# Expert weights in 16 KB runs, TensorE's order inside an expert turn rotated, the token copy split

## What is computed

```python
N_EXPERTS, TOP_K, EXPERT_FF = 32, 2, 512
# hier_moe: softmax over 4 groups, best group, two best experts in it; weights w
def expert_block(args):
    xblk, e = args
    return (jax.nn.silu(xblk @ w_gate[e]) * (xblk @ w_up[e])) @ w_down[e]
# the outputs, times their routing weights, are added up for each token
```

## Time and profile before

| | |
|---|---|
| median of 3 runs | 2574.07 us (2572.4 to 2574.95) |
| span of the profiled execution | 2569.7 us |
| mean granted TensorE clock | 0.941 |
| PE busy, DVE busy, ACT busy | 2164.8 us, 826.1 us, 386.2 us |
| HBM read, written | 606.41 MB, 30.93 MB |
| expert weight loads | 198 of 2048 KB |
| stores to `y_rows` from SBUF | 132 of 128 KB, 5.5 us to landing |
| L680 MATMUL (up) | x2112, 489.5 us busy, mean 617 ns |
| L699 MATMUL (down) | x1056, 241.2 us busy, mean 597 ns |
| L659 MATMUL (tokens) | x1696, 202.1 us busy, mean 280 ns |

### The profile page before, as it was taken

The page is one execution under the profiler, slowest core; times in us unless marked ns, Lnnn a source line. Parts: engine busy times, 40 slices in busy tenths (PEclk is TensorE's granted clock), DMA queues, the critical chain, the costliest instruction groups (busy, mean ns, idle before and its releaser), DMA issues. The chain is left out here.

```text
span 2569.7 us, 27407 instructions
## 1 busy us (share of the span) xinstructions
PE 2164.8 (84%) x10510; PEld 1378.6 (54%) x10514; DVE 826.1 (32%) x1726; ACT 386.2 (15%) x724; POOL 113.9 (4%) x56
## 2 busy tenths in 40 slices
PE   7789998978999893697999888885989788888874
PEld 6578887667888641444444444444546433333332
DVE  1456663045666529023111111113073311111112
ACT  1321111042111210420000000002122100000000
POOL 0000000000000008500000000001000000000000
PEclk9899999999999897898999999997989899999997
DMA  7536656312766643014999999987121599999994
GB/s 253 196 112 253 224 201 248 139 50 82 260 230 221 221 180 130 0 66 177 397 397 397 396 397 397 397 316 247 66 99 66 194 396 396 397 397 397 396 396 149
DMA packets 273636, 638.07 MB, mean 248 GB/s; under 512 B 7120, under 2 KB 10224, under 8 KB 273456
## 3 DMA queue, kind: packets, MB, share of 16 engines
q1 hardware_dynamic: 256096, 595.48, 62.3%
q0 software_dynamic: 5600, 21.27, 2.3%
q10 hardware_dynamic: 11888, 20.62, 2.2%
HBM read 606.41 MB, written 30.93 MB: 248 GB/s over the span
## 5 line engine op out<-in xcount | busy, mean ns | idle before, releaser
L680 PE MATMUL T<-ring,S 128*64 128x512 f32 x2112 | 489.5, 617 | 75.1 <-issue 68.8
L680 PEld LDWEIGHTS T<-ring,S 128*64 128x64 f32 x2112 | 179.9, 142 | 376.9 <-issue 373.8
L561 PE MATMUL T<-X,ring 128*128 128x256 f32 x1536 | 338.9, 380 | 0.0
L561 PEld LDWEIGHTS T<-X,ring 128*128 128x128 f32 x1536 | 292.4, 191 | 40.2 <-issue 0.6
L699 PE MATMUL T<-ring,S 128*64 128x512 f32 x1056 | 241.2, 597 | 40.1 <-DVE S L1465 40.1
L1463 DVE TENSOR_TENSOR S<-S,T 128x256 f32<-128x256 f32 x66 | 27.8, 422 | 727.5 <-ACT S L1056 727.5
L1267 DVE SCALAR_TENSOR_TENSOR S<-ring,cs,S 128x512 f32<-128x512 f32 x336 | 229.5, 745 | 0.0
L659 PEld LDWEIGHTS T<-S 128*128 128x128 f32 x1696 | 195.5, 195 | 41.3 <-issue 41.3
L659 PE MATMUL T<-S 128*128 128x128 f32 x1696 | 202.1, 280 | 14.3 <-DVE S L1346 14.3
L569 PE MATMUL T<-S,ring 128*128 128x256 f32 x768 | 176.7, 383 | 15.1 <-DVE S L1297 15.1
L506 PE MATMUL T<-H,ring 128*128 128x512 f32 (+1 forms) x496 | 167.7, 501 | 4.4 <-ACT H L1023 4.0
(11 more groups left out here) (269 smaller groups left out, 1565.6 us busy)
## 6 DMA issues: line engine op xcount, KB each, us to landing
ring<-in_exp_w_gate SPq DMA_DIRECT2D x66, 2048.0 KB, 18.6
ring<-in_exp_w_up SPq DMA_DIRECT2D x66, 2048.0 KB, 22.7
ring<-in_exp_w_down SPq DMA_DIRECT2D x66, 2048.0 KB, 19.9
ring<-in_ffn_w_up SPq DMA_DIRECT2D x24, 2048.0 KB, 12.7
ring<-in_mod_w SPq DMA_DIRECT2D x24, 2048.0 KB, 7.9
ring<-in_ffn_w_down SPq DMA_DIRECT2D x12, 2048.0 KB, 7.8
y_rows<-S ACTq DMA_DIRECT2D x132, 128.0 KB, 5.5
y_rows<-zb POOLq DMA_DIRECT2D x4, 3072.0 KB, 22.6
```

Of the source, the lines that this page charges most:

```text
L561: ins = pe.matmul(T[:, m % 2, h * S:(h + 1) * S], w[:, k, m * P:(m + 1) * P], x1[:, k, :], start=(k == 0), stop=(k == KT - 1))
L680: ins = pe.matmul(T[c * B:(c + 1) * B, s, :].rearrange("p (a n) -> p a n", a=2), xgT[:, k, s * B:(s + 1) * B], ring[:, 3 * s:3 * s + 2, k ...
```

## The change

- **Loads.** The DRAM side is read as `e (p k) n -> p (e k n)`: partition p takes rows 8p to 8p + 7 of gate and up (4p to 4p + 3 of down), 16 KB in one run. The bytes are the same.
- **Matching the new order of rows.** `hrow` is written permuted by ScalarE (input from PSUM with a step of 8 elements), so that token column q of tile k is input channel 8q + k. The up-projection reads its moving operand as `p g (q f) -> p g f q`: elements 16 bytes apart, so that hidden unit 4q + f comes out at column q of block f.
- **TensorE's order.** A prologue does tokens and the up-projection s = 0 of the first turn. The loop body is: transpositions (i, 0), tokens (i + 1), up (i, 1), down (i, 0), transpositions (i, 1), up (i + 1, 0), down (i, 1). An epilogue does the last turn without tokens. SyncE, ScalarE and VectorE follow the same order, with a prologue and an epilogue of their own; the count in `plan` is one lower.
- **Token copy.** The 128 x 1024 copy becomes two, one for each s, and semaphore `xT` counts two for each turn. GpSimd's wait for `xT_all` goes.

```diff
@@ -442,8 +442,8 @@
                 weights = (a["exp_w_gate"], a["exp_w_up"], a["exp_w_down"])
 
                 def load(m, w):
-                    src = w.rearrange("e (k p) n -> p (e k) n", p=P)
-                    sp_.dma_start(mslot(m, src.shape[1], src.shape[2]), src).then_inc(r["landed"][m], 16)
+                    src = w.rearrange("e (p k) n -> p (e k n)", p=P)
+                    sp_.dma_start(ring[:, m, :], src).then_inc(r["landed"][m], 16)
 
 
                 for m in (3, 4, 5, 2, 0, 1):
...
@@ -451,25 +451,37 @@
                     load(m, weights[m % 3][l][m // 3:m // 3 + 1])
                 sp_.wait_ge(r["planned"], l + 1)
                 t0 = first_turn(sp_, l)
-                t1 = end_turn(sp_, l, t0)
-
-                def expert(i, at, s):
-
-                    e = sp_.value_load(plan[0:1, l, ds(at * 2 + (1 + s), 1)], min_val=0, max_val=NE - 1)
-                    for j, w in enumerate(weights):
-
-                        if j < 2:
-                            sp_.wait_ge(r["m_full"], 2 * i + (s + 1))
-                        else:
-                            sp_.wait_ge(r["y_full"], 2 * i + (s + 1))
-                        load(3 * s + j, w[l][ds(e, 1)])
-
-                with sp_.Fori(t0 + 1, t1) as i:
+                tl = final_turn(sp_, l, t0)
+
+                def expert_of(i, s):
+
                     at = turn_of_layer(i, t0, l)
-                    for s in range(2):
-                        expert(i, at, s)
+                    return sp_.value_load(plan[0:1, l, ds(at * 2 + (1 + s), 1)], min_val=0, max_val=NE - 1)
+
+                def gate_up(i, s, e):
+
+                    sp_.wait_ge(r["m_full"], 2 * i + (s + 1))
+                    for j in range(2):
+                        load(3 * s + j, weights[j][l][ds(e, 1)])
+
+                def down(i, s, e):
+
+                    sp_.wait_ge(r["y_full"], 2 * i + (s + 1))
+                    load(3 * s + 2, weights[2][l][ds(e, 1)])
+
+                gate_up(t0 + 1, 0, expert_of(t0 + 1, 0))
+                with sp_.Fori(t0 + 1, tl) as i:
+                    a0, b0 = expert_of(i, 0), expert_of(i, 1)
+                    gate_up(i, 1, b0)
+                    down(i, 0, a0)
+                    gate_up(i + 1, 0, expert_of(i + 1, 0))
+                    down(i, 1, b0)
+                a0, b0 = expert_of(tl, 0), expert_of(tl, 1)
+                gate_up(tl, 1, b0)
+                down(tl, 0, a0)
+                down(tl, 1, b0)
                 if l == 0:
-                    sp_.wait_ge(r["y_full"], t1 * 2 + 2)
+                    sp_.wait_ge(r["y_full"], tl * 2 + 4)
                     for t in range(TT[0]):
                         sp_.wait_ge(r["cg"][t], 32)
...
@@ -652,8 +664,8 @@
 
                 def turn_tokens(i):
 
-                    pe.wait_ge(r["xT"], i + (l + 1))
-                    pe.wait_ge(r["oh"], i + (l + 1))
+                    pe.wait_ge(r["xT"], 2 * i + 1)
+                    pe.wait_ge(r["oh"], i + 1)
                     for k in range(KT):
                         for t in range(TT[l]):
                             ins = pe.matmul(T[:, 6 + k // 4, (k % 4) * P:(k % 4 + 1) * P],
...
@@ -661,44 +673,61 @@
                                             start=(t == 0), stop=(t == TT[l] - 1))
                     ins.then_inc(r["tr"], 1)
 
+                def up(i, s):
+
+                    pe.wait_ge(r["landed"][3 * s], 16 * i + 16)
+                    pe.wait_ge(r["landed"][3 * s + 1], 16 * i + 16)
+                    pe.wait_ge(r["xT"], 2 * i + (s + 2))
+                    for k in range(KT):
+                        w = ring[:, 3 * s:3 * s + 2, k * CH:(k + 1) * CH].rearrange("p g (q f) -> p g f q", f=MJ)
+                        for c in range(2):
+                            ins = pe.matmul(T[c * B:(c + 1) * B, s, :].rearrange("p (g f q) -> p g f q", g=2, f=2),
+                                            xgT[:, k, s * B:(s + 1) * B], w[:, :, 2 * c:2 * c + 2, :],
+                                            start=(k == 0), stop=(k == KT - 1))
+                    ins.then_inc(r["m_full"], 1)
+
+                def turn_hidden(i, s):
+
+                    pe.wait_ge(r["hm"], 2 * i + (s + 1))
+                    for j in range(2):
+                        ins = pe.transpose(T[:, 2, j * P:(j + 1) * P], hm[:, s, j * P:(j + 1) * P], ident)
+                    ins.then_inc(r["hT_full"], 1)
+
+                def down(i, s):
+
+                    pe.wait_ge(r["landed"][3 * s + 2], 16 * i + 16)
+                    pe.wait_ge(r["m_act"], 2 * i + (s + 1))
+                    pe.wait_ge(r["hT"], 2 * i + (s + 1))
+                    wd = mslot(3 * s + 2, MJ, D)
+                    for f in range(MJ):
+
+                        off = (f % 2) * P + (f // 2) * B
+                        for n in range(2):
+                            ins = pe.matmul(T[n * B:(n + 1) * B, 4 + s, :], hT[:, s, off:off + B],
+                                            wd[:, f, n * 512:(n + 1) * 512], start=(f == 0), stop=(f == MJ - 1))
+                    ins.then_inc(r["y_full"], 1)
+
                 for j in range(1, 5):
                     if 2 * TT[l] >= j:
                         read(pe, u0[f"rows{l}"] + 2 * TT[l] - j)
 
-
-
                 turn_tokens(t0)
+                up(t0, 0)
                 pe.wait_ge(r["planned"], l + 1)
-                t1 = end_turn(pe, l, t0)
-                with pe.Fori(t0, t1) as i:
-                    for s in range(2):
-                        pe.wait_ge(r["landed"][3 * s], 16 * i + 16)
-                        pe.wait_ge(r["landed"][3 * s + 1], 16 * i + 16)
-                        pe.wait_ge(r["xT"], i + (l + 2))
-                        for k in range(KT):
-                            for c in range(2):
-                                ins = pe.matmul(T[c * B:(c + 1) * B, s, :].rearrange("p (a n) -> p a n", a=2),
-                                                xgT[:, k, s * B:(s + 1) * B],
-                                                ring[:, 3 * s:3 * s + 2, k * CH + c * 256:k * CH + (c + 1) * 256],
-                                                start=(k == 0), stop=(k == KT - 1))
-                        ins.then_inc(r["m_full"], 1)
-                        if s == 1:
-                            turn_tokens(i + 1)
-                        pe.wait_ge(r["hm"], 2 * i + (s + 1))
-                        for j in range(2):
-                            ins = pe.transpose(T[:, 2, j * P:(j + 1) * P], hm[:, s, j * P:(j + 1) * P], ident)
-                        ins.then_inc(r["hT_full"], 1)
-                        pe.wait_ge(r["landed"][3 * s + 2], 16 * i + 16)
-                        pe.wait_ge(r["m_act"], 2 * i + (s + 1))
-                        pe.wait_ge(r["hT"], 2 * i + (s + 1))
-                        wd = mslot(3 * s + 2, MJ, D)
-                        for f in range(MJ):
-
-                            off = (f % 2) * P + (f // 2) * B
-                            for n in range(2):
-                                ins = pe.matmul(T[n * B:(n + 1) * B, 4 + s, :], hT[:, s, off:off + B],
-                                                wd[:, f, n * 512:(n + 1) * 512], start=(f == 0), stop=(f == MJ - 1))
-                        ins.then_inc(r["y_full"], 1)
+                tl = final_turn(pe, l, t0)
+                with pe.Fori(t0, tl) as i:
+                    turn_hidden(i, 0)
+                    turn_tokens(i + 1)
+                    up(i, 1)
+                    down(i, 0)
+                    turn_hidden(i, 1)
+                    up(i + 1, 0)
+                    down(i, 1)
+                turn_hidden(tl, 0)
+                up(tl, 1)
+                down(tl, 0)
+                turn_hidden(tl, 1)
+                down(tl, 1)
 
             def combine(l):
                 tt = TT[l]
...
@@ -1035,7 +1064,9 @@
                 evac(u, lgT[:, 0:tt * P], in_=bank(u, tt * P)[0:36, :])
                 nc.scalar.preload_act_table(ACT.Exp)
                 for j in range(2 * tt):
-                    evac(u0[f"rows{l}"] + j, hrow[:, j // 2, (j % 2) * 512:(j % 2 + 1) * 512])
+                    u = u0[f"rows{l}"] + j
+                    evac(u, hrow[:, j // 2, :].rearrange("p (k q) -> p k q", k=KT)[:, :, (j % 2) * 64:(j % 2 + 1) * 64],
+                         in_=bank(u).rearrange("p (q k) -> p k q", k=KT))
                 act.wait_ge(r["ge"], l + 1)
                 A(rt[:, 512:512 + 5 * tt], rt[:, 512:512 + 5 * tt], ACT.Exp).then_inc(r["gx"], 1)
...
@@ -1448,24 +1492,41 @@
             def experts(l):
                 t0 = first_turn(dve, l)
                 dve.wait_ge(r["planned"], l + 1)
-                t1 = end_turn(dve, l, t0)
-                def tokens(i):
-                    dve.wait_ge(r["tr"], i + (l + 1))
-                    V.tensor_copy(part(S1, 0, 2, 512), T[:, 6:8, :]).then_inc(r["xT"], 1)
-
-                tokens(t0)
-                with dve.Fori(t0, t1) as i:
+                tl = final_turn(dve, l, t0)
+
```

(96 more changed lines are left out.)

## The result

The changed kernel takes **2882.31 us** (median of 4 runs, 2879.28 to 2885.42) against 2573.76 us before: a ratio of 1.1199, with a 95% interval of 1.1184 to 1.1215. I had forecast 2498 us. The profiled execution has a span of 2883.5 us.

What follows compares the result with a forecast made beforehand. The weights' DMA was taken to bound both layers; gains of 39.3 us (layer 0) and 37.0 us (layer 1), together 76.3, 67 of it packet rate, took the 2569.7 us span to 2493.4, plus 4.4 to the median: 2498 us; range 2477 to 2536.

Steps and rivals of the forecast that it cites:

- Part 4: Up-projection's moving operand read with 16 bytes between elements: cost from zero to +14 us a turn, taken as zero.
- rival (b): Up-projection slowed by the strided operand: about 2855 us in total at x = 1; chance 0.04 mild, 0.14 beyond.
- beyond: Up-projections stretched past x = 0.39, where both layers are back at today's time; chance 0.14.
- x: Share by which up-projections stretch; a TensorE turn becomes 29.0 + 14x us in layer 0, 25.5 + 14x in layer 1.
- Part 1: Weight loads in 16 KB runs: DMA rate from 397 to 426 GB/s, a turn from 33.09 to 30.87 us.
- Rival (a): Weight loads: the DMA rate doesn't follow run length; 2531 us at 411 GB/s (chance 0.09), 2565 at 397 (0.04).
- Part 2: TensorE's new order: stalls of 0.93 and twice 0.61 us go in layer 0; worth little by itself, it makes room.
- the gap at the start: Start of each layer: third load waits for the second up-projection; DMA queue dry for 5.3 us in layer 0, 1.8 in layer 1.
- the room it makes: Layer 0: without the new order turns would stop at 31.18 us, losing 16 x 0.3 us = 5 us.
- Part 3: Split copy: two of about 0.7 us, first up-projection 0.6 us earlier; ScalarE's strided PSUM reads 0 to +3 us per layer, taken 0.
- A's figure: Expectation for the old order with the step, if the 16-byte step alone doubles the up-projection: total about 2960 us.

Runs made afterwards that it cites:

- the run with pairs: The changed kernel with the up-projection's moving operand read as two neighbouring f32, then a step of 16 bytes; all 16 KB runs kept: 2489.3 us, 0.9677 of before.

## Why the prediction was wrong

**What failed is one choice in Part 4**, the cost of the strided operand. The term was bounded from 0 to +14 us a turn and taken at zero; measured +14.9 (2 x 7.43), just past the upper end. That end came from the column rate at half the clock, and the clock had nothing to do with it (it was granted at 1.00): that it fits so well is luck. The reason given for zero was a false comparison. The bf16 row shows a reader that delivers an element every 0.53 ns (0.27 us for 512), and I set that against 0.86 ns for f32 (0.44 us for 512). Counted in 16-byte pieces, bf16 takes one every 4.2 ns and flat f32 one every 3.4. No row had ever asked for a piece in less; the step asks for one with every column, in 0.84 ns. The rows said nothing about what was needed, and the sentence of the Trainium skill in rival (b) did. The chance of 0.14 for "beyond" was too low for the same reason, and the range left that rival out.

**The price of rival (b) was right, given x.** At x = 1, the same upper end, it gave 2855 us. Measured is x = 14.42/6.99 - 1 = 1.06, and 0.06 x 462 = 28 us more makes 2883; the kernel took 2882. Its turns at x = 1 are 43.0 and 39.5 us; found were 43.84 and 40.28.

**Part 1** (the runs) holds in the run with pairs: 429 GB/s over a turn, where I had worked out 425, and 30.58 us instead of 30.87. Over 182 loads that is 182 x 0.29/6 = 8.8 us, the whole distance between 2498 and 2489. Rival (a), that the rate doesn't follow the length, falls.

**Part 2** (the order) holds: the stalls are gone, order alone came to 2564 us as expected ahead of that run, and the gap at the start is there. The worth of the room it makes was put too low: 5 us against 27 measured, since I set 31.18 against 30.87 and the real pair was 31.93 against 30.58: the pairs added 0.75 us to the turn of the old order, and the DMA was 0.29 us faster.

**Part 3** holds: the halves of the copy take 0.69 us each, and the first up-projection waits 0.88 us in layer 0 and 0.78 in layer 1, where it was 1.32: 0.4 to 0.5 us won, not 0.6. The stores took 8.0 us to landing instead of 5.5, under the cover of the turn. ScalarE's evacuations with a step of 32 bytes in PSUM:

```profile
1160.38 4.03 ACT L1058 ACTIVATE S<-T 128x512 f32<-128x512 f32 x8
```

4.03 us as in the earlier trace rows. So the 0 to 3 us there were 0.

## What to carry to other kernels

When a layout is changed so that transfers get longer, price what the readers then do: count the 16-byte pieces that a matmul's moving f32 operand touches per column, and keep two elements in each, by making the pair the innermost dimension. When a term is unknown and its bounds lie on different sides of the break-even, look for a row that asks as much of the same resource in the same unit; if there is none, the end that the Trainium skill supports deserves more than a remainder. A rotation that hides stalls is worth little under a DMA bound (7.5 us here) and should be judged together with the edit that lifts that bound.

## What the runs showed that I had not expected

ScalarE's PSUM reads at a step of 32 bytes are free (4.03 us for eight, as flat), while TensorE's SBUF reads of the moving operand at 16 bytes cost double.

The old order with the step lost more than the step. Its down-projections as a group, then one of them in layer 0 and the slowest, in layer 1, each after two short waits, and the sums of stretches around them (clock third from the end):

```profile
L703 PE MATMUL T<-ring,S 128*64 128x512 f32 x1056 | 283.9, 685 | 40.2 <-DVE S L1469 40.2
...
1436.54 5.20 PE L703 MATMUL T<-ring,S 128*64 128x512 f32 x16 [0.61 <-DVE S L1469]
...
2458.11 6.41 PE L703 MATMUL T<-ring,S 128*64 128x512 f32 x16 [0.61 <-DVE S L1469]
...
1436.54:1441.50 4.96, 4.96 (x16) 1.71 (x18) 0.00 (x0) 0.00 (x0) 0.00 (x0) 0.68 0.98 352
2441.30:2455.80 14.50, 14.50 (x34) 2.79 (x30) 0.00 (x0) 0.60 (x1) 0.00 (x0) 1.00 0.76 299
2455.80:2458.00 2.20, 0.77 (x4) 0.28 (x2) 0.85 (x2) 0.38 (x1) 0.00 (x0) 0.74 0.17 46
2458.11:2464.30 6.19, 6.19 (x16) 2.02 (x18) 0.00 (x0) 0.00 (x0) 0.00 (x0) 0.55 1.01 364
```

The granted clock was 1.00 (2.4 GHz) through the strided up-projection. It fell to 0.68, once to 0.55 (1.2 GHz for most of the stretch), after 0.93 and 0.61 us of waiting, so that in 26 of the 33 turns the first down-projection took 5.0 to 5.4 us, once 6.41, instead of 3.65; in the other seven it took 3.65. Over the run the down-projections are busy for 283.9 us, against 241.2 before: 43 of the 47 us above A's figure. The kernel before has the same two waits behind flat up-projections, and all its 66 down-projections took 3.65 us; the changed kernel has the strided reads without the waits, and its clock stayed at 1.00 too. For waits this short it took both together, and not even both always sufficed. Which of the two matters how much wasn't tried. Flat reads don't keep the clock through longer waits: in the run with the step undone an up-projection took 8.78 us instead of 7.09 after 2.11 us of waiting for its weights, with a clock of 0.65 over its first 4 us.
